# Delta rule on one core: solved coefficients spread by two matmuls in the weights' format

## The reference, cut to what matters

```python
m = jnp.where(strict, jnp.einsum("bhnid,bhnjd->bhnij", kb, k) * decay, 0.0)
a_mat = m + jnp.eye(CHUNK)
sol = lax.linalg.triangular_solve(a_mat, rhs, left_side=True, lower=True, unit_diagonal=True)
```

## Time and profile before

| | us |
|---|---|
| median of three runs | 2158.72 |
| the profiled execution | 2158.62 |
| its span, first to last instruction | 2156.6 |
| TensorE busy | 2141.2 |
| VectorE / ScalarE / GpSimd busy | 1088.3 / 1040.5 / 1712.4 |
| the four pairs of the delta rule | about 893 to 1270 of the span |

### The profile page before, as it was taken

One profiled execution on the slowest core, in us unless ns is written; L12 is line 12 of the kernel. 1 busy time (PEld: TensorE's weight loads), 2 busy tenths in 40 slices (PEclk: granted clock), 3 DMA queues, 4 the chain that ended last, 5 costly groups with the idle time before them and its releaser, 6 DMA issues.

```text
span 2156.6 us, 35027 instructions
## 1 busy us (share of the span) xinstructions
PE 2141.2 (99%) x12847; PEld 1842.1 (85%) x12847; DVE 1088.3 (50%) x1934; ACT 1040.5 (48%) x1533; POOL 1712.4 (79%) x729
## 2 busy tenths in 40 slices
PE   9999999999999999999999999999999999999998
PEld 8888889888888888888888888888888888888886
DVE  5994343115764263668586855118506704812832
ACT  5434455444566555636455654453333333333343
POOL 7888867877666886667686778888888888888886
PEclk9999999999999999999999999999999999999999
DMA  7666545656544765556565556666666666666664
GB/s 240 193 187 194 177 153 174 190 157 188 147 138 149 238 179 147 150 150 182 147 180 153 159 155 199 209 182 189 191 193 192 186 194 192 188 194 189 192 189 152
DMA packets 322773, 385.95 MB, mean 179 GB/s; under 512 B 15079, under 2 KB 256078, under 8 KB 322390
## 3 DMA queue, kind: packets, MB, share of 16 engines
q1 hardware_dynamic: 317269, 378.06, 59.0%
q10 hardware_dynamic: 5376, 6.11, 0.9%
HBM read 382.01 MB, written 2.11 MB: 178 GB/s over the span
## 4 chain that ended last, share of the span: by engine, by line
PE 96%; ACT 1%; DVE 1%; issue 1%; POOL 1%; DMA 0%; ACTq 0%; POOLq 0%; DVEq 0%
PE lin_ps L2238 37%; PE lin_ps L2241 18%; PE lin_ps L2264 10%; PE lin_ps L2265 10%; PE lin_ps L2266 10%; PE ps L2201 1%; PE lin_ps L2448 1%; PE lin_ps L2446 1%; PE lin_ps L2447 1%; POOL w_lo L643 1%; PE ps L2591 0%; DVE ps L1904 0%; PE lin_ps L2377 0%; PE lin_ps L2378 0%; PE lin_ps L2376 0%
## 5 line engine op out<-in xcount | busy, mean ns | idle before, releaser
L643 POOL TENSOR_TENSOR w_lo<-raw,w_hi 128x1024 fp32r<-128x1024 f32 (+1 forms) x712 | 1701.4, 2400 | 420.0 <-ACT w_hi L684 310.9
L2238 PE MATMUL lin_ps<-a,w_hi 128*128 128x512 f32 x2176 | 695.8, 401 | 1.6 <-issue 0.8
L684 ACT ACTIVATE w_hi<-raw 128x1024 fp32r<-128x1024 f32 (+1 forms) x452 | 470.7, 1053 | 444.2 <-PE lin_ps L2241 221.3
L2241 PEld LDWEIGHTS lin_ps<-a,w_lo 128*128 128x128 f32 x2176 | 408.7, 188 | 96.4
L2238 PE MATMUL lin_ps<-b,w_hi 128*128 128x512 f32 x1376 | 432.7, 396 | 0.8 <-DVE z L1552 0.8
L2241 PE MATMUL lin_ps<-a,w_lo 128*128 128x256 f32 x2176 | 428.3, 278 | 0.0
L695 ACT ACTIVATE w_hi<-raw 128x1024 fp32r<-128x1024 f32 x228 | 242.0, 1062 | 385.6 <-PE lin_ps L2241 226.4
L2238 PEld LDWEIGHTS lin_ps<-a,w_hi 128*128 128x128 f32 x2176 | 332.6, 189 | 7.8 <-issue 4.5
L2241 PEld LDWEIGHTS lin_ps<-b,w_lo 128*128 128x128 f32 x1376 | 258.5, 188 | 61.1
L2264 PE MATMUL lin_ps<-w_hi,a 128*128 128x512 f32 x752 | 293.3, 390 | 0.0
L2266 PE MATMUL lin_ps<-w_hi,a 128*128 128x512 f32 x752 | 292.7, 389 | 0.0
(11 more groups left out here) (435 smaller groups left out, 2127.0 us busy)
## 6 DMA issues: line engine op xcount, KB each, us to landing
raw<-in_w_in SPq DMA_DIRECT2D x144, 512.0 KB, 3.7
raw<-in_w_mlp_up SPq DMA_DIRECT2D x128, 512.0 KB, 3.8
raw<-in_w_mlp_down SPq DMA_DIRECT2D x128, 512.0 KB, 3.7
raw<-in_even_w_in SPq DMA_DIRECT2D x111, 512.0 KB, 4.4
raw<-in_odd_w_in SPq DMA_DIRECT2D x40, 512.0 KB, 3.7
raw<-in_even_w_out SPq DMA_DIRECT2D x32, 512.0 KB, 4.2
raw<-in_odd_w_out SPq DMA_DIRECT2D x32, 512.0 KB, 4.8
raw<-in_w_o SPq DMA_DIRECT2D x32, 512.0 KB, 4.2
```

Source lines behind the costliest of these rows:

```text
L643: nc.gpsimd.tensor_tensor(w_lo[:, slot, 0:width], raw[:, slot, 0:width], w_hi[:, slot, 0:width].bitcast(F32), ALU.subtract).then_inc(lo_do ...
L684: nc.scalar.activation(w_hi[:, slot, 0:width], raw[:, slot, 0:width], ACT.Copy).then_inc(hi_done, 1)
L2238: nc.tensor.matmul(lin_ps[:, 2 * parity + m, :], hi[:, k, m * P:(m + 1) * P], src[:, kk].rearrange("p s n -> p (s n)"), start=(q == 0 and ...
L2241: last = nc.tensor.matmul(lin_ps[:, 2 * parity + m, 0:T], lo[:, k, m * P:(m + 1) * P], src[:, kk, 0, :], start=False, stop=(q == n - 1 and ...
```

## The change

The 92 coefficients of a way are split: `rounded` is their value in the format `fp32r`, `w.rest` what is left, computed in PSUM. Both are placed into 480 columns, in two tiles `placed[0]` and `placed[1]` that lie in `b` and are shared by the two ways; `spread` becomes two matmuls of the format `fp32r` that add up, with `same_r`, the 0/1 matrix in that format. As the tiles are shared, way 1 waits on VectorE for the spread of way 0 (`mb`), and way 0 for that of way 1 in the pair before. All placements now stand behind the step `t3`. On TensorE `fill(9)`, both spreads, `fill(15)` become `fill(7)`, one spread, `fill(3)`, the other spread, `fill(14)`. In `inverses` the solved numbers are first copied to PSUM, and read from there. In the list of VectorE's steps (not shown) `vh`, `vl`, `lw0`, `lw1`, `lw2` follow `pl2`, and `sol` stands ahead of `ex0`.

```diff
--- before.py
+++ after.py
@@ -119,6 +119,7 @@
 FILL, FILL_G = IN2 + 32, IN2_G + 8
 BASE = 16
 HALF = BASE // 2
+N_VALUES = 4 * BASE + 4 * (HALF - 1)
 
 
 def _z_rows(k):
@@ -247,6 +248,9 @@
         opening = sb("opening", [P, 20])
         iw = sb("iw", [P, TT, IH])
         own5 = sb("own5", [P, 5, T])
+        spread_r = sb("spread_r", [P, P + 96], F32R)
+        same_r, rounded = spread_r[:, 0:P], spread_r[:, P:P + N_VALUES]
+        placed = [b[:, 6 + k].rearrange("p s n -> p (s n)")[:, 0:4 * HALF * (BASE - 1)] for k in range(2)]
         ikt = own5[:, 4, :]
 
 
@@ -361,8 +365,8 @@
...
@@ -429,7 +433,8 @@
                 self.r = self.decay
                 self.tu = both.rearrange("p (m n) -> p m n", m=8)
                 self.rhs = both
-                self.placed = both[:, 0:4 * HALF * (BASE - 1)].rearrange("p (n r j) -> p n r j", n=4, r=HALF)
+                self.values, self.rest = self.x_ps[:, 0:N_VALUES], self.x_ps[:, P:P + N_VALUES]
+                self.solved = self.x_ps[:, 0:4 * BASE].rearrange("p (n i) -> p n i", n=4)
                 self.coef = self.x_ps[:, 0:4 * HALF * (BASE - 1)].rearrange("p (n r j) -> p n r j", n=4, r=HALF)
                 self.t, self.u = self.tu[:, 0:4, :], self.tu[:, 4:8, :]
                 self.v_dec = self.t
@@ -1800,7 +1805,7 @@
             dve.wait_ge(mk, done("c"))
             nc.vector.tensor_tensor(same, in_block[:, 0], in_block[:, 1], ALU.add).then_inc(mk, 1)
             dve.wait_ge(mk, done("s"))
-            nc.vector.tensor_tensor(same, same, ident[:], ALU.add).then_inc(mk, 1)
+            nc.vector.tensor_tensor(same_r, same, ident[:], ALU.add).then_inc(mk, 1)
             nc.vector.tensor_scalar(in_block, in_block, -1.0, None, ALU.mult).then_inc(mk, 1)
             nc.vector.tensor_reduce(nth, ident[:].rearrange("p (b i) -> p i b", i=BASE), AX.X, ALU.add).then_inc(mk, 1)
             dve.wait_ge(mk, done("nth"))
@@ -1940,14 +1945,27 @@
                     for k, (ns, _, _, second, mark) in enumerate(halves_of):
                         after(w, f"t{k}")
                         nc.vector.scalar_tensor_tensor(out=w.ends[:, ns, :], in0=second, scalar=mark, in1=w.part[:, ns, :], op0=ALU.mult, op1=ALU.add).then_inc(own, 1)
-                    wide = [P, 2, HALF, HALF]
-                    for d, part, row in ((0, w.sums[:, 0:2, BASE - 1:HALF - 1:-1], nth[:, HALF - 1::-1]), (1, w.sums[:, 2:4, 0:HALF], nth[:, HALF:BASE])):
-                        nc.vector.tensor_tensor(w.placed[:, 2 * d:2 * d + 2, :, 0:HALF], part.unsqueeze(2).broadcast_to(wide),
-                                                row.unsqueeze(2).unsqueeze(1).broadcast_to(wide), ALU.mult).then_inc(own, 1)
+                    def place(half, sums, ends):
+                        out = placed[half].rearrange("p (n r j) -> p n r j", n=4, r=HALF)
+                        wide = [P, 2, HALF, HALF]
+                        for d, part, row in ((0, sums[:, 0:2, BASE - 1:HALF - 1:-1], nth[:, HALF - 1::-1]), (1, sums[:, 2:4, 0:HALF], nth[:, HALF:BASE])):
+                            nc.vector.tensor_tensor(out[:, 2 * d:2 * d + 2, :, 0:HALF], part.unsqueeze(2).broadcast_to(wide),
+                                                    row.unsqueeze(2).unsqueeze(1).broadcast_to(wide), ALU.mult).then_inc(own, 1)
+                        wide = [P, 4, HALF, HALF - 1]
+                        nc.vector.tensor_tensor(out[:, :, :, HALF:BASE - 1], ends.unsqueeze(2).broadcast_to(wide),
+                                                either.unsqueeze(2).unsqueeze(1).broadcast_to(wide), ALU.mult).then_inc(own, 1)
+
                     after(w, "t3")
-                    wide = [P, 4, HALF, HALF - 1]
-                    nc.vector.tensor_tensor(w.placed[:, :, :, HALF:BASE - 1], w.ends.unsqueeze(2).broadcast_to(wide),
-                                            either.unsqueeze(2).unsqueeze(1).broadcast_to(wide), ALU.mult).then_inc(own, 1)
+                    if w.w:
+                        dve.wait_ge(dn_pe[0].sem, dn_pe[0].at("mb", p))
+                    elif p:
+                        dve.wait_ge(dn_pe[1].sem, dn_pe[1].at("mb", p - 1))
+                    place(0, w.sums, w.ends)
+                    nc.vector.tensor_scalar(rounded, w.values, 1.0, None, ALU.mult).then_inc(own, 1)
+                    after(w, "vh")
+                    nc.vector.tensor_tensor(w.rest, w.values, rounded.bitcast(F32), ALU.subtract).then_inc(own, 1)
+                    after(w, "vl")
+                    place(1, w.rest[:, 0:4 * BASE].rearrange("p (n i) -> p n i", n=4), w.rest[:, 4 * BASE:N_VALUES].rearrange("p (n i) -> p n i", n=4))
 
                 def masked(w):
                     own, y = dn_dve[w.w].sem, four1(w.y_ps)
@@ -1979,8 +1997,10 @@
                 def inverses(w):
                     own = dn_dve[w.w].sem
                     after(w, f"su{BASE - 1}")
+                    nc.vector.tensor_scalar(w.solved, w.inv, 1.0, None, ALU.mult).then_inc(own, 1)
+                    after(w, "sol")
                     wide = [P, 2, P // BASE, BASE]
-                    for d, solved in ((0, w.inv[:, 0:2, ::-1]), (1, w.inv[:, 2:4, :])):
+                    for d, solved in ((0, w.solved[:, 0:2, ::-1]), (1, w.solved[:, 2:4, :])):
                         nc.vector.tensor_tensor(w.t[:, 2 * d:2 * d + 2, :].rearrange("p c (b i) -> p c b i", i=BASE), solved.unsqueeze(2).broadcast_to(wide),
                                                 which.unsqueeze(2).unsqueeze(1).broadcast_to(wide), ALU.mult).then_inc(own, 1)
 
@@ -2725,8 +2745,9 @@
 
                 def spread(w):
                     from_dve(w, "qk")
-                    nc.tensor.matmul(w.x_ps[:, 0:4 * HALF * (BASE - 1)], same, w.placed.rearrange("p n r j -> p (n r j)"),
-                                     start=True, stop=True).then_inc(dn_pe[w.w].sem, 1)
+                    for half in range(2):
+                        m = nc.tensor.matmul(w.x_ps[:, 0:4 * HALF * (BASE - 1)], same_r, placed[half], start=(half == 0), stop=(half == 1))
+                    m.then_inc(dn_pe[w.w].sem, 1)
 
                 def squares(l, n):
 
@@ -2807,10 +2828,11 @@
                 fill(3)
                 grams(one_way)
                 grams(other)
-                fill(9)
+                fill(7)
                 spread(one_way)
+                fill(3)
                 spread(other)
-                fill(15)
+                fill(14)
                 for l, ready, n in ((4, "tt1", 2), (5, "l43", 2), (6, "l53", 1)):
                     level(l, ready)
                     fill(n)
```

More of the change, by code:

```diff
@@ L363, in build @@
         dn_dve = [steps(f"dn_dve{w}", [f"cv{y}{k}" for k in range(NT) for y in range(3)]
-                        + ["ks", "rn", "dsub0", "dsub1", "dsub2", "dsub3", "dmin", "m0", "m1", "m2", "m3", "blk", "red", "t0", "t1", "t2", "t3", "pl0", "pl1", "pl2", "qk", "mm4", "one0", "one1", "x0"]
-                        + [y for n in range(1, BASE) for y in (f"pr{n}", f"su{n}")] + ["ex0", "ex1", "tt0", "tt1"]
+                        + ["ks", "rn", "dsub0", "dsub1", "dsub2", "dsub3", "dmin", "m0", "m1", "m2", "m3", "blk", "red", "t0", "t1", "t2", "t3", "pl0", "pl1", "pl2", "vh", "vl", "lw0", "lw1", "lw2", "qk", "mm4", "one0", "one1", "x0"]
+                        + [y for n in range(1, BASE) for y in (f"pr{n}", f"su{n}")] + ["sol", "ex0", "ex1", "tt0", "tt1"]
                         + [f"l{l}{n}" for l in (4, 5) for n in range(4)] + ["u60", "u61", "vd0", "vd1", "v10", "v11", "ra", "rb", "v20", "v21",
```

## The result

The changed kernel takes 2166.30 us (median of seven runs, 2163.99 to 2167.45) against 2158.72: the ratio is 1.0031, with a 95% interval of 1.0022 to 1.0041. It is slower by 7.6 us, inside the range and on the side that was forecast, with 2.3 us more than the forecast of 2164.0. The profiled execution is one of 2166.30 us, with a span of 2164.4 us.

What follows compares the result with a forecast made beforehand. TensorE bounds the kernel, and VectorE's added work delays what half unit 24 needs. 4 x 2.74 - 6.24 + 4 x 0.16 = 5.4 us slower, 2158.6 + 5.4 = 2164.0; range 2160.0 to 2166.6.

Steps and rivals of the forecast that it cites:

- The place: TensorE stands idle behind each pair's second spread, before half unit 24, until VectorE ends `group_out(7p+1)`: 1.5 us, 2.8 in pair 0.
- Rival A: VectorE keeps up and only TensorE's saving counts: 2156.0 us; chance 0.11 with its half-way versions.
- D: VectorE's added work for both ways of a pair, ahead of `group_out(7p+1)`: 2.74 us, bounds 2.36 to 3.20.
- B: Rival: the spread's passes on TensorE are no cheaper than before, each of four takes 0.80 us: 2165.9 us; chance 0.03.
- C: Rival: way 1's wait on `mb` becomes late as spread 0 is held up: 2168 with 1 us a pair; chance 0.03.
- The price: Each pair costs D less its cover, plus the restart: 5.4 us slower in all, 2.2, 1.0, 1.0, 1.1 by pairs.
- cover: Time from the end of `group_out(7p+1)` on VectorE to half unit 24's start on TensorE: 0.69 to 1.88 us, together 6.24.
- restart: TensorE's added time when it starts again after a wait for an accumulator half: 0.16 us in each pair.
- TensorE's own saving: Two-pass `fp32r` spreads save TensorE 0.64 us a pair, 2.6 in all, but this is spent in the wait.
- What costs nothing: ScalarE's `keep_m` of way 1 moves by D; `inverses` gets shorter behind 5.3 us of cover; neither was to reach TensorE.

Runs made afterwards that it cites:

- e5: The kernel before with VectorE making each way's placements three times, all behind `t3`, and TensorE unchanged: 2165.69 us, ratio 1.0036.
- e1: The changed kernel with the split of the fills taken back to `fill(9)`, both spreads, `fill(15)`: 2174.28 us, ratio 1.0075.
- e9: The kernel of e3 with ScalarE's `keep_m` of way 1 moved behind the rounding of unit 16: 2155.10 us, ratio 0.9984 against the kernel before.
- e6: The changed kernel with `inverses` reading the solved numbers from SBUF as before, no copy to PSUM: 2164.81 us, ratio 1.0029.
- e3: The changed kernel with `group_out(7p+1)` moved between the two ways and fills of 7, 5 and 12 half units: 2158.66 us, ratio 1.0000.
- e2: The changed kernel with `group_out(7p+1)` moved between the two ways and nothing else: 2165.16 us, ratio 1.0035.
- e8: The changed kernel with the edits of e3 in pairs 1 to 3 only, pair 0 left as it is: 2161.22 us, ratio 1.0012.

## Why the prediction was right

- **The place.** Right: the wait is at half unit 24 in every pair, behind the second spread, ended by `group_out`. In pairs 1 to 3 the spread itself does not wait; in pair 0 it waits 0.55 us, which the prediction allowed for. Rival A fell with D, which is more than twice its limit of 1.2 us, and with e5, B with the spreads' 0.44 us for two passes (1014.54 to 1014.98), and C is kept off by the split, as e1 shows.
- **The size of D.** 2.74 forecast, 2.84 measured. The placements took 0.70, `rounded` 0.24 and the rest 0.26 us. The formula for PSUM that the prediction quoted from the Trainium skill (VectorE: DVE Perf Modes, section The TRN2 errata) makes an estimate of 0.221 us for each of the last two. The trace disagrees, by 0.02 and 0.04 us. The 0.245 that the prediction took from rows was nearer.
- **The price.** D less cover plus restart: 5.4 forecast; found in the trace 5.7 up to half unit 24 of pair 3, 2.2, 1.1, 1.2 and 1.2 by pairs, and 5.9 with the restart behind it. The three runs of the changed kernel without a lower mean clock have a median of 2164.30, against 2164.0 forecast.
- **What was left out.** The restart was priced as 0.16 us in each pair, from a place where TensorE had waited 0.4 us. Behind pair 0's gap of 0.55 and 1.95 us it cost 1.6 us more where the clock fell. This is the term that was mis-sized; it moved the median to the upper end of the range. The forecast's own upper bound was 2165.8, so the median lies above that; that it is still inside the range, by 0.3 us, is luck, as the range's end was set with rival B in mind and not with the clock.
- **TensorE's own saving.** 0.64 a pair forecast, 0.74 found in e9. The two added changes between kinds of matmul cost nothing that shows.
- **What costs nothing.** `inverses`: right, by e6. ScalarE's `keep_m`: right for the changed kernel, where TensorE waited for VectorE anyway; wrong as soon as that wait was gone (e3), since `mm4` is later by another 1.9 us there.

What stays open: in e2 and e6 some runs at a mean clock of 0.999 are as long as some at 0.998, and e5 has runs 2.9 us apart that are all at 0.999. Only one execution of each was profiled, so how much of their spread is the step can't be said.

## What to carry to other kernels

An engine that is half idle can still have no time to spare at one point: find the instruction of the busy engine that waits for it next, and measure from the end of what it waits for to its start. Work added ahead of that point costs its length less that cover, and a release of a buffer that stands behind other work in the same engine's order is the first to come late. When one wait is taken away, look at once for the queue behind the instruction that moved, as the second wait here (ScalarE's copy ahead of four roundings) was worth as much as the gain.

## What was not expected of the hardware

A gap of 0.55 and 1.95 us with one spread between them (TensorE busy 1.83 of 4.00 us) was followed by a granted clock of 0.50 in some executions, four of seven by the mean clock, and single gaps of 1.6 us in pairs 1 to 3 by none in the profiled one. In e1, where each pair has one gap of up to 2.8 us at the second spread, the profiled execution shows it behind all four. But in e2 the 2.4 us ahead of pair 0's second spread, and in e8 pair 0's 0.5 and 2.0 us, were followed by a granted clock of 1.00 in the profiled executions. So the length of a gap alone does not tell whether the clock falls behind it. The Trainium skill, in TensorE: Matmul & The Clock Gate, section HAM oscillation, tells of a clock that falls after idle stretches and takes back time from the work behind them; the trace of the changed kernel agrees, with 1.6 us for one step.
